# A chunked scan's triangular inverse: the last two doubling steps on small array tiles

## The chip, the cores and the metric

The kernel runs on one core of a Trainium2 chip, in float32 throughout. The metric is the device time of one execution in microseconds (us). A core has TensorE (PE in the profile; its weight loads are rows of their own, PEld), VectorE (DVE), ScalarE (ACT), GpSimd (POOL) and SyncE (SP), each with its own stream of instructions; they wait for each other through semaphores.

## The reference

The reference is two transformer-like blocks one after the other. The change lies in the first layer of the first block, in the part that computes the RWKV-7 recurrence of 8 heads of width 64 over 512 tokens (256 of context, 256 latent), once forwards and once backwards:

```
def step(S, r, w, k, v, a, b):
    S = S * w + (S @ a) outer b + v outer k      # one token
    y = S @ r
```

The kernel does not go token by token. It takes chunks of 128 tokens, and for each chunk and head it needs the inverse of a unit triangular matrix, (I - A)^-1, with A strictly triangular, 128x128. A is made of inner products of decayed keys.

## The kernel before, in words

**Units.** The scan is 16 units (`UNITS`): 2 directions x 4 chunks x 2 groups of four heads. One turn of the loop `for u, (d, c, pg) in enumerate(UNITS)` does unit u and prepares unit u+1. The same loop is written out three times, for PE, ACT and DVE, by hand; the order in each stream is the order of the code, and the semaphores `pe_done`, `act_done`, `vec_done` tell the engines how far the others are. SP issues no transfer that the scan waits for.

**The inverse.** All four heads of a unit are worked on, in two pairs p = 0 and 1. `ED` holds powers of the part of A inside 16x16 diagonal blocks, `TD` the growing inverse T; each has a plain half and a transposed half. `squared` and `grown` give the inverse within blocks of 16 (T1, T2, T4, T8). Then three doubling steps, lv = 0, 1, 2, go from blocks of 16 to 32, from 32 to 64 and from 64 to 128. Before the change each of them is the same: `bridge_mask` (DVE, L2451) multiplies A's transpose `dm` by a constant mask that leaves only the blocks which this step brings in, giving `bm[lv]`. `bridge` (PE, L983) multiplies that with T over the full 128x128 (Z, to banks 7 and 2), `bridge_out` (ACT, L1794) copies Z from PSUM to `zt`. `merged` (PE, L991, through `grown`, L970) multiplies Z with T, again over 128x128, and for lv = 1 in both the plain and the transposed form. `merged` on DVE (L2442) adds the product to T and writes it into the other buffer of `TD`. PE's pairs alternate: while ACT copies p = 0, PE computes p = 1.

A function `two` issues two products; each product of float32 operands is two weight loads and two matmuls in the trace. So `bridge` of one step and pair is 4 matmul records, at line L961, where `two` stands.

**Around it on PE, in one unit.** After step 0 come the products for x (L1036, L1041), then step 1, then `grams_a(u + 1)` (L949, four products of the next unit, at L955, with 64-row tiles), then step 2, then L1061 and L1065, and L1074, the first user of the finished inverse. On DVE, `masked` (L2388, rows at L2392), `masked_a` (L2396, rows at L2399) and `diagonal` (L2412) of the next unit stand between the steps. `bridge_mask(u + 1, 1)` and `bridge_mask(u + 1, 2)` stand at the end of the unit, behind the state (L2518) and ahead of the next unit's first `grown`.

Of the kernel before, what the change touches and what calls it, by code (L numbers as in the profile page):

```python
# [24 lines left out]
P = 128  # L25
# [195 lines left out]
class Counts:  # L221
# [16 lines left out]
    def at(self, engine, name):  # L238
        return 1 if self.known is None else self.known[engine, name]
# [12 lines left out]
def build(nc, w, out, counts, stop="end"):  # L252
# [5 lines left out]
    with ExitStack() as ctx:  # L258
# [137 lines left out]
        bm = [take(m, 4, P) for m in ("w0", "v", "ring 1")]  # L396
        zt = take("v", 4, P)
        POWER_BANK, GROW_BANK = (7, 2), (3, 4)

        def half_of(t, i, p, half):  # L400
            return cut(t[i][:, p, :], 256 * half, 2, P)
# [225 lines left out]
        def _(pe):  # L627
# [331 lines left out]
            def two(b, o, lhs, rhs):  # L959
                for m in range(2):  # L960
                    i = mm(bank[b][:, o + P * m:o + P * m + P], lhs[:, m, :], rhs[:, m, :],  # L961
                           start=True, stop=True, skip_group_check=True)
                return i
# [16 lines left out]
                for p in range(2):  # L980
                    squared("E2", u, p, 0)

            def bridge(u, lv, p):  # L983

                if p == 0:
                    pe.wait_ge(vec_done, at(VE, ("bm", u, lv)))
                pe.wait_ge(vec_done, at(VE, (("T8 turned", u, p), ("Tm turned", u, 0, p), ("Tm", u, 1, p))[lv]))
                two(POWER_BANK[p], 0, bm[lv][:, 2 * p:2 * p + 2, :], half_of(TD, 1 - lv % 2, p, 1)
                    ).then_inc(pe_done, did(PE, ("Z", u, lv, p)))

            def merged(u, lv, p):  # L991

                pe.wait_ge(act_done, at(AC, ("Z", u, lv, p)))
                z = zt[:, 2 * p:2 * p + 2, :]
                grown(("Tm", lv), u, p, z, 1 - lv % 2, ((0,), (0, 1), (1,))[lv])

            decays(0)
            by_token(0)
# [3 lines left out]
            for u, (d, c, pg) in enumerate(UNITS):  # L1002
# [21 lines left out]
                if not last:  # L1024
                    grams(u + 1)
                for p in range(2):
                    bridge(u, 0, p)
                for p in range(2):
                    merged(u, 0, p)


                pe.wait_ge(vec_done, at(VE, ("sin", u)))
# [13 lines left out]
                for p in range(2):  # L1046
                    bridge(u, 1, p)
                for p in range(2):
                    merged(u, 1, p)
                if not last:  # L1050
                    grams_a(u + 1)
                for p in range(2):
                    bridge(u, 2, p)
                for p in range(2):
                    merged(u, 2, p)


                if not last:
# [11 lines left out]
                for q in range(2):  # L1070
                    pe.wait_ge(vec_done, at(VE, ("Tm", u, 2, q)))
# [534 lines left out]
        def _(ac):  # L1606
# [55 lines left out]
            def copy(name, dst, src, scale=1.0):  # L1662
                act(dst, src, ACT.Copy, scale=scale).then_inc(act_done, did(AC, name))  # L1663
# [130 lines left out]
            def bridge_out(u, lv):  # L1794

                for p in range(2):
                    ac.wait_ge(pe_done, at(PE, ("Z", u, lv, p)))
                    copy(("Z", u, lv, p), zt[:, 2 * p:2 * p + 2, :], cut(bank[POWER_BANK[p]], 0, 2, P))

            decays(0)  # L1800
            out_of("bkt", 0, 5, bkt[0])
# [1 line left out]
            for u in range(len(UNITS)):  # L1803
                last = u + 1 == len(UNITS)
                if not last:
                    decays(u + 1)
                power_out("E4", u, 0)
                power_out("E8", u, 1)
                if not last:
                    out_of("bkt", u + 1, 5, bkt[(u + 1) % 2])  # L1810
                bridge_out(u, 0)
                ac.wait_ge(pe_done, at(PE, ("x", u)))
                copy(("xs", u), xs, cut(bank[0], 0, 2, P))
                bridge_out(u, 1)
                bridge_out(u, 2)
# [230 lines left out]
        def _(ve):  # L2046
# [395 lines left out]
            def merged(u, lv, p, before):  # L2442

                ve.wait_ge(vec_done, before)
                ve.wait_ge(pe_done, at(PE, (("Tm", lv), u, p)))
                o, e = ((0, 256), (0, 512), (256, 512))[lv]
                i = 1 - lv % 2
                V.tensor_tensor(TD[1 - i][:, p, o:e], TD[i][:, p, o:e], bank[GROW_BANK[p]][:, o:e], ALU.add
                                ).then_inc(vec_done, did(VE, ("Tm", u, lv, p)))

            def bridge_mask(u, lv):  # L2451

                off = wide(const(("off32", "off64", "off128")[lv])[:, None, :], 4, P)
                V.tensor_tensor(bm[lv], dm[u % 2], off, ALU.mult).then_inc(vec_done, did(VE, ("bm", u, lv)))

            for part in range(5):
                decayed(0, part)
# [5 lines left out]
            diagonal(0, 1)  # L2463
            for p in range(2):
                power_turned("E2", 0, p, 1)
            for lv in range(3):
                bridge_mask(0, lv)
            for u, (d, c, pg) in enumerate(UNITS):
                last = u + 1 == len(UNITS)
                grown("T2", u, 0, 0, at(VE, ("T1", u)))  # L2470
                power_turned("E4", u, 0, 0)
                if not last:
                    decayed(u + 1, 0)
                grown("T2", u, 1, 0, at(VE, ("T1", u)))
                power_turned("E4", u, 1, 0)
                if not last:
                    decayed(u + 1, 1)
                grown("T4", u, 0, 1, at(VE, ("T2", u, 0)))
                grown("T4", u, 1, 1, at(VE, ("T2", u, 1)))
                if not last:  # L2480
                    decayed(u + 1, 2)
                if not last:
                    decayed(u + 1, 3)
                for p in range(2):
                    grown("T8", u, p, 0, at(VE, ("T4", u, p)))
                    inverse_turned(("T8 turned", u, p), u, p, 1, at(VE, ("T8", u, p)))
                if not last:
                    decayed(u + 1, 4)
                if not last:
                    masked(u + 1, 0)  # L2490
                for p in range(2):
                    merged(u, 0, p, at(VE, ("T8", u, p)))
# [3 lines left out]
                for p in range(2):  # L2496
                    merged(u, 1, p, at(VE, ("Tm turned", u, 0, p)))
# [4 lines left out]
                for p in range(2):  # L2502
                    merged(u, 2, p, at(VE, ("Tm", u, 1, p)))
                if not last:
                    diagonal(u + 1, 1)
                    bridge_mask(u + 1, 0)
                    for p in range(2):
                        power_turned("E2", u + 1, p, 1)
                ve.wait_ge(pe_done, at(PE, ("s", u)))
                op(("s sum", u), V.tensor_tensor(stt_, sin_[u % 2], cut(bank[6], 0, 2, P), ALU.add))  # L2510
                for jj in range(2):
                    V.scalar_tensor_tensor(state[:, 4 * d + 2 * pg + jj, :], stt_[:, jj, :],
                                           ex[u % 2][:, jj, 257:258], const("head"), ALU.mult, ALU.mult
                                           ).then_inc(vec_done, did(VE, ("state 1" if jj else "state 0", u)))
                ve.wait_ge(pe_done, at(PE, ("y", u)))
                y_ = yt[:, c, 256 * pg:256 * pg + 256]
                if d == 0:
                    V.tensor_copy(y_, bank[5][:, 0:256]).then_inc(vec_done, did(VE, ("state", u)))  # L2518
# [426 lines left out]
```

## Time and profile before

| | |
|---|---|
| median of 3 runs | 3063.39 us (3062.32 to 3063.72) |
| the profiled execution, span from first to last instruction | 3062.6 us |
| runs' median beyond that span | 0.8 us |
| PE busy | 2955.8 us (97%) |
| one scan unit, period | 22.25 us |
| scan, units | 16, from about 340 to 697 us |

The profile is of one execution. A row of the timeline joins neighbouring instructions of an engine that have the same line and operands: its start, the time to the end of the last one, the engine, the line, the operation, and the count. What is in brackets is idle time of the engine ahead of the row and what ended it. A PE row's shape "128\*128" is the rows and columns of the array that its weights fill; "128x128" behind it is the moving operand and result.

### The profile page before, as it was taken

What the parts mean: (1) busy time and instruction counts of PE and PEld (TensorE: products, weight loads), DVE (VectorE), ACT (ScalarE), POOL (GpSimd) and SP (SyncE); (2) the same over time, 40 slices, a digit from 0 to 9 for tenths busy, and PEclk for the clock granted to TensorE, in tenths of its full rate; (3) what the DMA queues carried; (4) which work ended last, traced back from release to release, by engine and by line L of the source; (5) the groups of instructions that cost most, each with busy time, mean ns of one, the idle gap of its engine ahead of it and who ended that gap; (6) DMA issues with size and microseconds to landing.
All of it is one profiled execution on the core that took longest, in us unless ns stands there. A gap on an engine that the chain in (4) does not pass through costs nothing.

```text
span 3062.6 us, 50591 instructions
## 1 busy us (share of the span) xinstructions
PE 2955.8 (97%) x21484; PEld 1949.8 (64%) x21484; DVE 1315.0 (43%) x3016; ACT 541.7 (18%) x1202; POOL 14.0 (0%) x13
## 2 busy tenths in 40 slices
PE   7999899999999999999899999999999899999998
PEld 5554699994344444557754555544568678877887
DVE  1567888875998987404421111111121432023211
ACT  2213332321211111204300000000011310022000
POOL 0000100000000000000000000000000000000000
PEclk8999899999999999999999999999999999999999
DMA  7232001004777885320299999999962235522551
GB/s 270 95 138 82 1 1 42 1 15 132 230 237 232 246 255 181 135 82 15 84 358 384 378 371 372 374 396 382 377 241 97 83 97 151 151 83 69 151 151 55
DMA packets 351380, 551.02 MB, mean 180 GB/s; under 512 B 14304, under 2 KB 292192, under 8 KB 347840
## 3 DMA queue, kind: packets, MB, share of 16 engines
q1 hardware_dynamic: 351168, 547.89, 51.2%
q8 instruction: 170, 2.79, 0.4%
q14 instruction: 42, 0.34, 0.0%
HBM read 546.80 MB, written 1.05 MB: 179 GB/s over the span
## 4 chain that ended last, share of the span: by engine, by line
PE 91%; DVE 4%; ACT 2%; DMA 1%; issue 1%; SPq 0%; ACTq 0%; DVEq 0%
PE bank L678 16%; PE bank L1367 15%; PE bank L1159 8%; PE bank L1383 8%; PE bank L1560 7%; PE bank L961 7%; PE bank L1173 5%; PE bank L757 3%; PE bank L637 3%; PE bank L1200 2%; PE bank L1104 2%; PE bank L945 1%; DVE mix L2143 1%; PE bank L1234 1%; PE bank L1326 1%; PE bank L1315 1%
## 5 line engine op out<-in xcount | busy, mean ns | idle before, releaser
L678 PE MATMUL bank<-a,ring 128*128 128x256 f32 (+1 forms) x1792 | 451.5, 414 | 9.2 <-DVE a L2078 6.6
L2143 DVE SCALAR_TENSOR_TENSOR mix<-arena,csil,mix 128x256 f32<-128x256 f32 x1008 | 402.1, 482 | 31.3 <-ACT mix L1663 31.3
L678 PEld LDWEIGHTS bank<-a,ring 128*128 128x128 f32 x1792 | 340.7, 191 | 116.8 <-issue 64.6
L1367 PE MATMUL bank<-ring,arena 128*32 128x352 f32 x5376 | 402.1, 459 | 1.7 <-DVE small L2681 1.7
L1367 PEld LDWEIGHTS bank<-ring,arena 128*32 128x32 f32 x5376 | 179.5, 110 | 218.8 <-issue 194.8
L1159 PE MATMUL bank<-a,ring 128*128 128x512 f32 x704 | 307.6, 597 | 6.8 <-ACT a L1659 6.8
L1159 PEld LDWEIGHTS bank<-a,ring 128*128 128x128 f32 x704 | 133.2, 191 | 179.9 <-issue 177.9
L1560 PE MATMUL bank<-arena,ring 128*128 128x256 f32 x1024 | 223.5, 379 | 2.0 <-DVE arena L2865 2.0
L1383 PE MATMUL bank<-ring,arena 128*32 128x256 f32 x3840 | 213.3, 379 | 0.0
L1560 PEld LDWEIGHTS bank<-arena,ring 128*128 128x128 f32 x1024 | 194.4, 190 | 29.1 <-DVE arena L2865 2.8
L2748 DVE TENSOR_TENSOR arena<-arena,bank 128x352 f32<-128x352 f32 x48 | 25.0, 521 | 433.7 <-ACT arena L1932 433.7
L1663 ACT ACTIVATE arena<-bank 128x256 f32<-128x256 f32 (+1 forms) x303 | 128.0, 429 | 365.2 <-PE bank L961 137.2
L1383 PEld LDWEIGHTS bank<-ring,arena 128*32 128x32 f32 x3840 | 125.3, 110 | 82.3 <-issue 3.7
L1173 PE MATMUL bank<-arena,ring 128*128 128x512 f32 x352 | 152.6, 593 | 1.5 <-DVE arena L2557 1.5
L2846 DVE TENSOR_SCALAR tmpA<-bank,mods 128x256 f32<-128x256 f32 x32 | 15.5, 484 | 288.0 <-PE bank L1560 213.9
L961 PE MATMUL bank<-arena 128*128 128x128 f32 x896 | 125.4, 285 | 3.9 <-DVE arena L2420 2.1
L1173 PEld LDWEIGHTS bank<-arena,ring 128*128 128x128 f32 x352 | 66.7, 190 | 86.4 <-issue 84.1
L961 PEld LDWEIGHTS bank<-arena 128*128 128x128 f32 x896 | 110.1, 193 | 16.5 <-ACT arena L1663 7.7
L1612 ACT ACTIVATE mix<-a 128x256 f32<-128x256 f32 x64 | 21.9, 417 | 526.5 <-DVE a L2058 526.5
L1663 ACT ACTIVATE mix<-arena,csil 128x256 f32<-128x256 f32 x144 | 64.2, 498 | 238.5 <-DMA arena<-in_ada_w 144.4
L757 PE MATMUL bank<-a,ring 128*128 128x512 f32 (+1 forms) x224 | 99.0, 594 | 0.0
L2861 DVE TENSOR_SCALAR tmpA<-bank 128x256 f32<-128x256 f32 x64 | 27.2, 425 | 164.3 <-PE bank L678 164.3
(422 smaller groups left out, 3203.4 us busy)
## 6 DMA issues: line engine op xcount, KB each, us to landing
ring<-in_moe_w SPq DMA_DIRECT2D x224, 704.0 KB, 9.2
ring<-in_moe_w SPq DMA_DIRECT2D x160, 512.0 KB, 6.5
ring<-in_mlp_w SPq DMA_DIRECT2D x64, 1024.0 KB, 5.5
arena<-in_ada_w SPq DMA_DIRECT2D x96, 512.0 KB, 3.7
arena<-in_w_ada SPq DMA_DIRECT2D x48, 512.0 KB, 3.6
ring<-in_ffn_w SPq DMA_DIRECT2D x22, 1024.0 KB, 8.4
arena<-in_moe_w SPq DMA_DIRECT2D x32, 704.0 KB, 10.0
h<-in_w_ada SPq DMA_DIRECT2D x8, 2048.0 KB, 7.6
```

What stands on the lines that cost most here:

```text
L637: i = mm(bank[b][:, 0:tile.shape[-1]], const("mean"), tile, start=(k == 0), stop=(k == KT - 1))
L678: i = mm(bank[b][:, 0:n], ws[:, k, t * P:t * P + P], rhs[:, k, sl], start=(k == 0), stop=(k == KT - 1))
L757: i = mm(bank[RKV_BANK[n]][0:m, :], ws[:, k, n % 2 * P:n % 2 * P + m], aT[:, k, :], start=(k == 0), stop=(k == KT - 1), skip_group_check=True)
L961: i = mm(bank[b][:, o + P * m:o + P * m + P], lhs[:, m, :], rhs[:, m, :], start=True, stop=True, skip_group_check=True)
L1104: i = mm(bank[MIX_BANKS[j % 5]], ws[:, k, j % 2 * P:j % 2 * P + P], src, start=(k == 4), stop=(k == 3), skip_group_check=True)
L1159: i = mm(bank[2 * t + i_], ws[:, k, t * P:t * P + P], aT[:, k, :], start=(k == 0), stop=(k == KT - 1))
L1173: i = mm(bank[2 + n % 4], ws[:, k, :], G[:, k, :], start=(k == 0), stop=(k == FT - 1))
L1367: i = mm(b[32 * t:32 * t + 32, 0:PART], ac_[:, g, 32 * k:32 * k + 32], by_tile(ws[i_], t), start=(k == 0), stop=(k == KT - 1), skip_group_ ...
L1383: i = mm(bank[Y_BANKS[g]][32 * q:32 * q + 32, 0:256], gT[:, p, g, 32 * c:32 * c + 32], ws[:, 256 * q:256 * q + 256], start=(n == 0), stop= ...
L1560: j = mm(bank[4 + n % 2][:, 0:TL], ws[:, k, :], G2[:, 16 * half + k, :], start=(half + k == 0), stop=(half * k == 15))
L1663: act(dst, src, ACT.Copy, scale=scale).then_inc(act_done, did(AC, name))
L2143: ins = V.scalar_tensor_tensor(dst, x, cond, dst, ALU.mult, ALU.add)
```

## The change

Step 0 stays as it was. Steps 1 and 2 are replaced. T after step 0 has nonzero blocks only in 32x32 diagonal blocks, and what step 1 adds to it is two 32x32 blocks; step 2 adds one 64x64 block. `blocks_of` gives, for a level, the pairs (on, by) of row and column ranges. `bridge_blocks` multiplies only such blocks of `dm` (no mask) and T; `merged_blocks` multiplies only the blocks of T and Z. `block_products` issues the four heads of one block pair one after the other, all on the same array tile. For step 1 the rows and columns are 32 wide: 8 products for Z, 12 for T (8 of one form, 4 of the transposed form of the first block, which step 2 needs). For step 2 they are 64 wide: 4 and 4. The four heads go to one PSUM bank, so there is no longer a pair p = 0 and a pair p = 1: one semaphore count tells that all of Z is done, and one that all of T's products are. ACT copies Z's blocks (two copies for step 1, one for step 2). DVE copies the new blocks into their place in the same buffer of `TD` (three copies for step 1, one for step 2), with no addition. The masks `bm` for steps 1 and 2 and their buffers go.

```
-            def bridge(u, lv, p):
+            def bridge(u, p):
...
+            def block_products(b, out_rows, out_cols, lhs, rhs):
+                for h in range(4):
+                    i = mm(bank[b][out_rows, P * h + out_cols.start:P * h + out_cols.stop], lhs(h), rhs(h),
+                           start=True, stop=True, skip_group_check=True)
+                return i
...
+            def bridge_blocks(u, lv):
+                if lv == 1:
+                    for p in range(2):
+                        pe.wait_ge(vec_done, at(VE, ("Tm turned", u, 0, p)))
+                else:
+                    pe.wait_ge(vec_done, at(VE, ("Tm", u, 1)))
+                for by, on in blocks_of(u, lv):
+                    i = block_products(BRIDGE_BANK[lv], on, by, lambda h: dm[u % 2][by, h, on],
+                                       lambda h: inverse_at(h, 1, by, by))
+                i.then_inc(pe_done, did(PE, ("Z", u, lv)))
+
+            def merged_blocks(u, lv):
+                pe.wait_ge(act_done, at(AC, ("Z", u, lv)))
+                for by, on in blocks_of(u, lv):
+                    i = block_products(4, on, by, lambda h: inverse_at(h, 0, on, on), lambda h: zt[on, h, by])
+                if lv == 1:
+                    by, on = blocks_of(u, 1)[0]
+                    i = block_products(3, by, on, lambda h: zt[on, h, by], lambda h: inverse_at(h, 0, on, on))
+                i.then_inc(pe_done, did(PE, ("Tm", u, lv)))
...
+            def bridge_blocks_out(u, lv):
+                ac.wait_ge(pe_done, at(PE, ("Z", u, lv)))
+                for n, (by, on) in enumerate(blocks_of(u, lv)):
+                    copy(("Z", u, lv) if n == 2 - lv else ("Z part", u, lv), zt[on, :, by],
+                         cut(bank[BRIDGE_BANK[lv]], 0, 4, P)[on, :, by])
...
+            def merged_blocks(u, lv):
+                ve.wait_ge(pe_done, at(PE, ("Tm", u, lv)))
+                pieces = [(1, 4, on, by) for by, on in reversed(blocks_of(u, lv))]
+                if lv == 1:
+                    by, on = blocks_of(u, 1)[0]
+                    pieces.insert(1, (0, 3, by, on))
+                for n, (half, b, rows_, cols_) in enumerate(pieces):
+                    V.tensor_copy(whole(TD, 0, half)[rows_, :, :, cols_], cut(bank[b], 0, 2, 2, P)[rows_, :, :, cols_]
+                                  ).then_inc(vec_done, did(VE, ("Tm", u, lv) if n + 1 == len(pieces)
+                                                           else ("Tm part", u, lv, n)))
...
-                if not last:
-                    bridge_mask(u + 1, 1)
-                    bridge_mask(u + 1, 2)
                 ve.wait_ge(vec_done, now(VE))
```

How the streams stand now. On PE, between the products for x and the first user of the finished inverse, before (two instructions of the trace for each product):

```order
L1036 MATMUL bank<-ring 128x128
L1041 MATMUL bank<-arena,h 128x64 x2
L961 MATMUL bank<-ring,arena 128x128 x6
L961 MATMUL bank<-arena,ring 128x128 x2
L961 MATMUL bank<-ring,arena 128x128 x2
L961 MATMUL bank<-arena,ring 128x128 x2
L955 MATMUL bank<-arena 128x128 x4
L961 MATMUL bank<-arena,ring 128x128 x4
L961 MATMUL bank<-arena 128x128 x4
L1061 MATMUL bank<-ring 128x128
```

and the same place in the changed kernel, where L1077 is the old L1036, L964 the old L955 and L1098 the old L1061:

```order
L1077 MATMUL bank<-ring 128x128
L1082 MATMUL bank<-arena,h 128x64 x2
L1008 MATMUL bank<-ring 32x32 x8
L1008 MATMUL bank<-arena,ring 32x32 x8
L1008 MATMUL bank<-ring,arena 32x32 x4
L964 MATMUL bank<-arena 128x128 x4
L1008 MATMUL bank<-ring 64x64 x4
L1008 MATMUL bank<-arena,ring 64x64 x4
L1098 MATMUL bank<-ring 128x128
```

The 12 products of step 1 and the 8 of step 2 have become 20 and 8. None has moved past another group.

On DVE, from the next unit's masked products to the end of the unit, before:

```order
L2392 TENSOR_TENSOR arena<-bank,consts 128x512 x2
L2448 TENSOR_TENSOR arena<-ring,bank 128x512 x2
L2399 TENSOR_TENSOR arena<-bank,consts 128x256 x2
L2416 TENSOR_TENSOR arena<-arena,consts 128x2x256
L2448 TENSOR_TENSOR ring<-arena,bank 128x256 x2
...
L2518 COPY ring<-bank 128x256
L2454 TENSOR_TENSOR arena<-arena,consts 128x512
L2454 TENSOR_TENSOR ring<-arena,consts 128x512
L2434 TENSOR_TENSOR arena<-ring,bank 128x256
```

and now, where L2500 is the new copy, L2442 the old L2399, L2459 the old L2416 and L2477 the old L2434:

```order
L2435 TENSOR_TENSOR arena<-bank,consts 128x512 x2
L2500 COPY ring<-bank 32x2x2x32 x3
L2442 TENSOR_TENSOR arena<-bank,consts 128x256 x2
L2459 TENSOR_TENSOR arena<-arena,consts 128x2x256
L2500 COPY ring<-bank 64x2x2x64
...
L2568 COPY ring<-bank 128x256
L2477 TENSOR_TENSOR arena<-ring,bank 128x256
```

The two additions of each step have become three copies and one, and the two masks (L2454) ahead of the next unit's first addition are gone.

## Rows read from the trace of the kernel before

**Rows 1.** The page, part 1: busy time, share of the span, instructions.

```profile
PE 2955.8 (97%) x21484; PEld 1949.8 (64%) x21484; DVE 1315.0 (43%) x3016; ACT 541.7 (18%) x1202; POOL 14.0 (0%) x13
```

**Rows 2.** Busy time by engine in a stretch of one unit.

```profile
core 0: us, PE busy (x) PEld busy (x) DVE busy (x) ACT busy (x) POOL busy (x), PEclk, DMA share, GB/s
409.60:431.90 22.30, 22.22 (x186) 20.65 (x185) 18.58 (x44) 7.03 (x20) 0.00 (x0) 1.00 0.01 2
```

**Rows 3.** Waits in the unit from 409.2 to 431.4: total us, times, longest.

```profile
ACT arena L1663 <- PE bank L961: 7.8, 6, 3.0
PEld bank L961 <- ACT arena L1663: 0.7, 3, 0.2
```

**Rows 4.** Timeline of PE's weight loads, steps 1 and 2 of that unit.

```profile
420.23 0.97 PEld L961 LDWEIGHTS bank<-ring,arena 128*128 128x128 f32 x8
421.43 0.52 PEld L961 LDWEIGHTS bank<-ring,arena 128*128 128x128 f32 x4 [0.22 <-ACT arena L1663]
...
422.76 0.53 PEld L961 LDWEIGHTS bank<-arena,ring 128*128 128x128 f32 x4
423.41 0.52 PEld L955 LDWEIGHTS bank<-arena 64*128 64x128 f32 x8
...
425.24 0.97 PEld L961 LDWEIGHTS bank<-arena 128*128 128x128 f32 x8 [0.22 <-ACT arena L1663]
426.12 0.30 PEld L1061 LDWEIGHTS bank<-ring 128*128 128x128 f32 x2
```

**Rows 5.** Timeline of DVE in the same unit, with one row of ACT's (420.99).

```profile
409.19 0.42 DVE L2518 COPY ring<-bank 128x256 f32<-128x256 f32 x1
409.53 0.68 DVE L2454 TENSOR_TENSOR arena<-ring,consts 128x512 f32<-128x512 f32 x1
410.12 0.68 DVE L2454 TENSOR_TENSOR ring<-ring,consts 128x512 f32<-128x512 f32 x1
410.84 0.42 DVE L2434 TENSOR_TENSOR arena<-ring,bank 128x256 f32<-128x256 f32 x1
...
420.06 0.45 DVE L2440 STREAM_TRANSPOSE ring<-ring 128x256 f32<-128x256 f32 x1
...
420.99 0.83 ACT L1663 ACTIVATE arena<-bank 128x256 f32<-128x256 f32 x2
...
422.69 0.69 DVE L2448 TENSOR_TENSOR arena<-ring,bank 128x512 f32<-128x512 f32 x1 [1.01 <-PE bank L961]
426.06 0.87 DVE L2448 TENSOR_TENSOR ring<-arena,bank 128x256 f32<-128x256 f32 x2 [0.52 <-PE bank L961]
...
431.44 0.42 DVE L2518 COPY ring<-bank 128x256 f32<-128x256 f32 x1
```

**Rows 6.** Groups by form, the scan from 343.9 to 697: count, busy us, mean ns.

```profile
L961 PE MATMUL bank<-ring,arena 128*128 128x128 f32 x508 | 75.0, 280 | 0.5
L1663 ACT ACTIVATE mix<-bank 128x256 f32<-128x256 f32 x32 | 12.3, 384 | 81.1 <-PE bank L1074 47.7 <-PE bank L1041 33.4
L1781 ACT ACTIVATE arena<-bank 128x128 f32<-128x128 f32 x28 | 7.9, 284 | 0.0
L2384 DVE TENSOR_SCALAR ring<-mix,arena 128x128 f32<-128x128 f32 x30 | 6.6, 264 | 0.0
```

**Rows 7.** Narrow weights elsewhere: a page group of the expert stage, and a timeline.

```profile
L1383 PE MATMUL bank<-ring,arena 128*32 128x256 f32 x3840 | 213.3, 379 | 0.0
...
L1383 PEld LDWEIGHTS bank<-ring,arena 128*32 128x32 f32 x3840 | 125.3, 110 | 82.3 <-issue 3.7
...
792.96 1.07 PE L1135 MATMUL bank<-mix,consts 128*32 128x512 f32 x8
792.96 0.16 PEld L1135 LDWEIGHTS bank<-mix,consts 128*32 128x32 f32 x8 [0.76 <-DVE mix L2143]
```

**Rows 8.** The same view, from 763 us on: a pause of PE, and the stretch behind it.

```profile
763.00:767.00 4.00, 0.74 (x2) 0.00 (x0) 2.53 (x2) 0.63 (x1) 0.00 (x0) 1.00 1.08 366
767.00:773.80 6.80, 3.28 (x4) 1.51 (x5) 6.42 (x9) 4.52 (x10) 0.00 (x0) 0.51 1.10 349
```

More of the change, by code:

```diff
@@ L395, in build, with blocks_of @@
         TD = [take(m, 2, 512) for m in ("ring 1", "lora")]
-        bm = [take(m, 4, P) for m in ("w0", "v", "ring 1")]
+        bm = take("w0", 4, P)
         zt = take("v", 4, P)
         POWER_BANK, GROW_BANK = (7, 2), (3, 4)
+        BRIDGE_BANK = (None, 7, 2)
+        def blocks_of(u, lv):
+            n, late = 32 * lv, UNITS[u][0] == 0
+            pairs = [(slice(2 * n * b + n, 2 * n * b + 2 * n), slice(2 * n * b, 2 * n * b + n))
+                     for b in range(P // (2 * n))]
+            return pairs if late else [(on, by) for by, on in reversed(pairs)]
         def half_of(t, i, p, half):
@@ L981, in squares @@
                     squared("E2", u, p, 0)
-            def bridge(u, lv, p):
+            def bridge(u, p):
                 if p == 0:
[L986 to L995, printed above, removed]
+                    pe.wait_ge(vec_done, at(VE, ("bm", u)))
+                pe.wait_ge(vec_done, at(VE, ("T8 turned", u, p)))
+                two(POWER_BANK[p], 0, bm[:, 2 * p:2 * p + 2, :], half_of(TD, 1, p, 1)
+                    ).then_inc(pe_done, did(PE, ("Z", u, 0, p)))
@@ new lines, in merged, with inverse_at @@
+            def merged(u, p):
+                pe.wait_ge(act_done, at(AC, ("Z", u, 0, p)))
+                grown(("Tm", 0), u, p, zt[:, 2 * p:2 * p + 2, :], 1)
+            def block_products(b, out_rows, out_cols, lhs, rhs):
[3 more added lines that the diff above has]
+                return i
+            def inverse_at(h, half, rows_, cols_):
+                return half_of(TD, 0, h // 2, half)[rows_, h % 2, cols_]
@@ L1026, in _ @@
                 for p in range(2):
-                    bridge(u, 0, p)
+                    bridge(u, p)
                 for p in range(2):
-                    merged(u, 0, p)
+                    merged(u, p)
                 pe.wait_ge(vec_done, at(VE, ("sin", u)))
@@ L1045, in _ @@
                 i.then_inc(pe_done, did(PE, ("x", u)))
[L1046 to L1049, printed above, removed]
+                bridge_blocks(u, 1)
+                merged_blocks(u, 1)
                 if not last:
                     grams_a(u + 1)
[L1052 to L1055, printed above, removed]
+                bridge_blocks(u, 2)
+                merged_blocks(u, 2)
                 if not last:
@@ L1069, in _ @@
                 pe.wait_ge(act_done, at(AC, ("xs", u)))
-                for q in range(2):
-                    pe.wait_ge(vec_done, at(VE, ("Tm", u, 2, q)))
+                pe.wait_ge(vec_done, at(VE, ("Tm", u, 2)))
                 for jj in range(2):
@@ L1792, in power_out, with bridge_out @@
                     copy((name, u, p), ED[i][:, p, 0:256], bank[POWER_BANK[p]][:, 0:256])
-            def bridge_out(u, lv):
+            def bridge_out(u):
                 for p in range(2):
-                    ac.wait_ge(pe_done, at(PE, ("Z", u, lv, p)))
-                    copy(("Z", u, lv, p), zt[:, 2 * p:2 * p + 2, :], cut(bank[POWER_BANK[p]], 0, 2, P))
+                    ac.wait_ge(pe_done, at(PE, ("Z", u, 0, p)))
+                    copy(("Z", u, 0, p), zt[:, 2 * p:2 * p + 2, :], cut(bank[POWER_BANK[p]], 0, 2, P))
+            def bridge_blocks_out(u, lv):
[3 more added lines that the diff above has]
+                         cut(bank[BRIDGE_BANK[lv]], 0, 4, P)[on, :, by])
             decays(0)
@@ L1810, in _ @@
                     out_of("bkt", u + 1, 5, bkt[(u + 1) % 2])
-                bridge_out(u, 0)
+                bridge_out(u)
                 ac.wait_ge(pe_done, at(PE, ("x", u)))
                 copy(("xs", u), xs, cut(bank[0], 0, 2, P))
-                bridge_out(u, 1)
-                bridge_out(u, 2)
+                bridge_blocks_out(u, 1)
+                bridge_blocks_out(u, 2)
                 ac.wait_ge(pe_done, at(PE, ("u", u)))
@@ L2440, in inverse_turned, with merged, bridge_mask @@
                 V.transpose(TD[i][:, p, 256:512], TD[i][:, p, 0:256]).then_inc(vec_done, did(VE, name))
-            def merged(u, lv, p, before):
+            def merged(u, p, before):
                 ve.wait_ge(vec_done, before)
[L2445 to L2454, printed above, removed]
+                ve.wait_ge(pe_done, at(PE, (("Tm", 0), u, p)))
+                V.tensor_tensor(TD[0][:, p, 0:256], TD[1][:, p, 0:256], bank[GROW_BANK[p]][:, 0:256], ALU.add
+                                ).then_inc(vec_done, did(VE, ("Tm", u, 0, p)))
+            def merged_blocks(u, lv):
[8 more added lines that the diff above has]
+                                                           else ("Tm part", u, lv, n)))
+            def bridge_mask(u):
+                V.tensor_tensor(bm, dm[u % 2], wide(const("off32")[:, None, :], 4, P), ALU.mult
+                                ).then_inc(vec_done, did(VE, ("bm", u)))
             for part in range(5):
@@ L2465, in _ @@
                 power_turned("E2", 0, p, 1)
-            for lv in range(3):
-                bridge_mask(0, lv)
+            bridge_mask(0)
             for u, (d, c, pg) in enumerate(UNITS):
@@ L2491, in _ @@
                 for p in range(2):
-                    merged(u, 0, p, at(VE, ("T8", u, p)))
+                    merged(u, p, at(VE, ("T8", u, p)))
                     inverse_turned(("Tm turned", u, 0, p), u, p, 0, at(VE, ("Tm", u, 0, p)))
@@ L2495, in _ @@
                     masked(u + 1, 1)
-                for p in range(2):
-                    merged(u, 1, p, at(VE, ("Tm turned", u, 0, p)))
+                merged_blocks(u, 1)
                 if not last:
@@ L2501, in _ @@
                     diagonal(u + 1, 0)
-                for p in range(2):
-                    merged(u, 2, p, at(VE, ("Tm", u, 1, p)))
+                merged_blocks(u, 2)
                 if not last:
                     diagonal(u + 1, 1)
-                    bridge_mask(u + 1, 0)
+                    bridge_mask(u + 1)
                     for p in range(2):
```

## The prediction

> **What bounds the kernel now.** I read the page first: PE is busy for 97% of the span [rows 1]. That alone doesn't say that fewer products are worth anything, so I went to the scan. One of its units, read between two copies of the same kind on DVE, lasts 431.44 - 409.19 = 22.25 us [rows 5]. In such a stretch PE is busy for 22.22 of 22.30 us, DVE for 18.58 and ACT for 7.03, at the full granted clock of 2.4 GHz (1.00) [rows 2]. The waits say the same from the other side: ACT waits for PE 7.8 us in a unit, while PE's weight loads wait for ACT 0.7 us [rows 3]. So PE's stream sets the scan's time, and a product taken from it is worth its own pace unless a wait takes its place.
>
> That pace: eight loads of 128 columns take 0.97 us, of which the last alone is 0.19, so a record follows the one before by (0.97 - 0.19) / 7 = 0.11 us [rows 4]. Loading hides behind multiplying. The stretch that the change rewrites runs from the first load of step 1 at 420.23 to the first load of L1061 at 426.12: **5.89 us** in each unit, 26% of it. In it are 40 records of the two steps (4.5 us), eight of L955, two waits for ACT of 0.22 us, and two changes of tile shape. A change costs 0.20 us: the loads at 422.76 end at 423.29, the next of the same shape would have begun 0.08 us before that end, and the one of L955 begins 0.12 after it [rows 4].
>
> **What is removed and what is added.** Of PE, 20 products of 128x128 (40 records) go, and 20 of 32x32 and 8 of 64x64 come (56 records). No operation with a 32x32 or 64x64 tile is in the trace, so their pace is the unknown. Its lower bound is what 32 columns take. At L1383 four column tiles work at once, each record of 256 columns comes 213.3 / 3840 = 0.0555 us after the last, so one tile streams 256 columns in 0.222 us and 32 columns in 0.028 [rows 7]. Weights of 32 columns don't ask for more: at L1135 eight loads for four tiles take 0.16 us, two to a tile [rows 7]. The upper bound that the rows of busy tiles allow is 0.0555 us, since L1383 proves that the queue can issue load and matmul at least so often. I take 0.028: at L1135 the eight loads, each 0.11 long, begin within 0.16 - 0.11 = 0.05 us, so the issue itself can be faster still. For 64 columns it is 0.056.
>
> The other prices. A result is there when its matmul ends: 0.28 us at 128 columns, 0.38 at 256 [rows 6, 7], so 0.20 at 32 and 0.23 at 64. From an engine's end to the next one's start I count 0.04 to 0.05 us: ACT's first copy begins at 420.99 and takes 0.38, and the load that waits for it begins at 421.43 [rows 4, 5]. A copy on ACT takes 0.28 us for 128 elements of each partition and 0.38 for 256 [rows 6]; on DVE 0.42 for 256 from PSUM [rows 5], and for 128 between 0.26 (from SBUF) [rows 6] and 0.42; I take 0.29, since 512 elements (0.69) and 256 (0.42) differ by 0.27 [rows 5], which makes 0.13 for 128 elements less. A second copy behind a first one, of the same engine, adds 0.17 on ACT and 0.21 on DVE, because it starts before the first ends, as the two masks do (0.59 apart at 0.68 each) [rows 5]. That only 32 or 64 partitions take part saves nothing.
>
> **The new stretch step by step**, in us of the same unit:
>
> - Step 1 now needs both pairs of T at once. DVE ends the second transposition at 420.51 [rows 5], so the first load is at 420.56 instead of 420.23 and the first matmul at 420.59. (The change of shape, 0.20, lies inside this wait.) Z, 16 records: last one 0.42 later, 421.01, result 421.21.
> - ACT's two copies: 421.25 to 421.70. PE loads at 421.75. Here PE stands still for 0.7 us; before, the second pair filled this.
> - T's products, 24 records from 421.78: last 422.42, result 422.62. DVE's three copies: 422.66 to 423.37.
> - L955: a change of shape, first load 422.54, matmuls from 422.65 to 422.99. It hides part of DVE's copies. The next load would be at 423.19; it waits for DVE until 423.42.
> - Z of step 2, 8 records from 423.47: last 423.86, result 424.09. ACT 424.13 to 424.51. PE loads at 424.56, its second long pause.
> - T's products of step 2: 424.61 to 425.00, a change of shape, and L1061's load at **425.15** instead of 426.12.
>
> So 4.5 us of records become about 2.0, the pauses on PE grow by some 1.3 us (0.33 at the start, 0.7 and 0.5 for ACT, 0.23 for DVE, less the two of 0.22), one more change of shape is seen, and the unit gains **0.97 us**. Does anything else take it back? DVE's copy of the last block ends at about 425.7; L1074 wants it at 425.15 + 1.34 = 426.49. DVE loses two masks of 0.68 each, and of its additions (1.38 and 0.87 busy) what the copies (0.71 and 0.42) don't take, over 2 us of 18.6: it can't become the bound. The masks stood ahead of the next unit's first addition at 410.84, which began with no idle time before it [rows 5]. PE hardly waited for that addition, so I count 0.03 us for their going, between 0 and 0.1. Together 1.0 us in each of 16 units: **16 us**. Behind the scan everything hangs on its end, and its transfers are released by it, so the gain arrives whole. The profiled execution would go from 3062.6 to 3046.6 us; its span lies 0.8 below the median of the runs, so the median goes from 3063.4 to **3047.4 us**.
>
> One rule speaks for a smaller gain. The Trainium skill (TensorEngine Tiling, Key Properties) says that changing the tiling mode drains TensorE; the trace agrees, with the 0.20 us above, and two changes in a unit become four. In my chain the two new ones fall into waits or are counted.
>
> **Rivals.**
>
> *Tiles overlap (3037 us).* The four heads of a block share one array tile, but the next block has another. L1135 runs its four tiles side by side (8 records of 0.59 us in 1.07 [rows 7]), where neighbours in the program are on different tiles. If PE also reaches past four products of one tile, Z of step 1 lasts 8 records instead of 16 and T's products 8 instead of 24: 24 x 0.028 = 0.67 us less, 1.65 in a unit, 26.4 us. Against it: nothing in this trace shows it reach so far. The TensorE page (Part 3, The mechanism) has matmuls in strict order and only loads pulled ahead, which would forbid it.
>
> *A floor on small records (about 3063 us).* If a 32x32 record takes 0.0555 us, the 15 + 23 steps between them cost 1.04 us more and nothing is left: 0.0 a unit. The skill (TensorE: Matmul & The Clock Gate, Wait — 56ns, not 53.3ns?) has a floor of 62 ns for a matmul that its sequencer handles in software; that mechanism here would be 38 x 0.034 = 1.3 us a unit more than my sum, 3068 us. The eight loads of L1135 that begin within 0.05 us speak against a floor. Of this rival's chance I give a quarter to that rule.
>
> *Records of one tile don't overlap (slower, about 3097 us).* Every tiled product of the kernel before has a neighbour on another tile. If, on one small tile, a load can't be hidden behind the matmul before it, a record takes the whole load of 32 columns, 0.110 us [rows 7]. Then 38 x 0.082 = 3.1 us a unit come on top: 2.1 us slower, 34 in all. It decides from 0.064 us a record on. Against it: at 128*128 the neighbours do share a tile, and there 0.11 is less than the 0.19 of a load.
>
> *The clock.* PE was granted 1.2 GHz (0.51) after a stretch in which it worked for 0.74 of 4.00 us [rows 8]. The new pauses are 0.7 us at most with work between them, yet a 32x32 tile is little work. A fifth of each unit at half clock would cost over 2 us and undo the gain.
>
> **How the numbers follow.** My forecast has 45%, the overlapping tiles 22%, the floor 17%, the tile without overlap 10%, the clock 6%. A measurement of this kernel can tell 0.2%, 6 us, from no change. The first two are faster (with a tail of the floor at 0.04 us a record): 0.71. The floor is the same: 0.15. The last two: 0.14. The range must leave out no more than two in ten: 3035, just past the overlapping tiles, to 3067, past the floor.
>
> **What would show it.** The period between the DVE copies should be 21.2 us. Rows of 32x32 records should have 16 in about 0.6 us and 24 in about 0.85; an ACT wait of PE of about 0.5 us, twice; a DVE wait ahead of the 64x64 products of 0.2. Records 0.055 or 0.11 us apart prove the rivals, and 16 records in 0.4 us the overlap. The masks' rows should be 16, not 48. The granted clock should stay at 1.00.

## The result, and the profile after

| | before | after |
|---|---|---|
| median | 3062.86 us (3061.47 to 3063.72, 4 runs) | 3126.41 us (3125.38 to 3128.35, 4 runs) |
| ratio, 95% interval | | 1.0209 (1.0196 to 1.0221): slower, by about 2% |
| span of the profiled execution | 3062.6 us | 3124.0 us |
| mean granted clock, share of full speed | 0.986 | 0.958 |
| mean period of a scan unit | 22.12 us | 25.81 us |

The change makes the kernel 63.6 us slower by the medians, where 16 us faster was forecast. Each of the 16 units ends with DVE writing y: a copy in the first eight (L2568), an addition in the others (L2570). Of the 61.4 us by which the spans differ, 55.3 lie between the first and the last of these 16 writes (387.1 instead of 331.8 us), 1.3 ahead of them and 4.8 behind, where the clock is low for 60.0 us instead of 46.1.

The page of the changed kernel, busy times and the granted clock in 40 slices (the first of these answers to [rows 1]; the scan is in slices 5 to 10):

```profile
PE 2992.2 (96%) x21740; PEld 1982.5 (63%) x21740; DVE 1283.2 (41%) x2984; ACT 531.3 (17%) x1186; POOL 14.0 (0%) x13
...
PEclk8999878878999999999989999999999999999999
```

PE is busy *longer* than before, 2992.2 against 2955.8 us, although 40 wide records of each unit gave way to 56 small ones. The slices that read 7 and 8 say why. The same in windows, columns as in [rows 2]: two neighbouring stretches of one unit, then 320 us of the scan.

```profile
391.90:405.40 13.50, 12.62 (x131) 11.46 (x131) 10.02 (x25) 4.81 (x14) 0.00 (x0) 1.00 0.01 1
405.50:419.00 13.50, 13.03 (x76) 12.44 (x72) 6.44 (x15) 1.53 (x4) 0.00 (x0) 0.50 0.00 1
...
340.00:660.00 320.00, 300.88 (x2470) 279.95 (x2469) 204.19 (x499) 79.38 (x225) 0.00 (x0) 0.81 0.03 11
```

In the first stretch PE runs at 2.4 GHz and does 131 records; in the second it is *more* busy (13.03 of 13.50 us) and does 76, in part of other kinds, at 1.2 GHz. The clock falls around step 1 or 2 of a unit and comes back some 7 to 14 us later. Between the first and the last of the DVE writes it is low for 156.6 us, in the kernel before for none. PE's weight loads show the price of a product at both levels. Those of the changed kernel, first eight 128x128 loads in a low stretch, then those of steps 1 and 2 in a unit at full clock, answering to [rows 4]:

```profile
413.70 1.83 PEld L970 LDWEIGHTS bank<-arena 128*128 128x128 f32 x8
...
482.39 0.48 PEld L1008 LDWEIGHTS bank<-ring 32*32 32x32 f32 x16 [0.32 <-DVE ring L2483]
483.62 0.41 PEld L1008 LDWEIGHTS bank<-arena,ring 32*32 32x32 f32 x14 [0.76 <-ACT arena L1699]
...
484.29 0.52 PEld L964 LDWEIGHTS bank<-arena 64*128 64x128 f32 x8
485.37 0.54 PEld L1008 LDWEIGHTS bank<-ring 64*64 64x64 f32 x8 [0.55 <-DVE ring L2500]
486.51 0.54 PEld L1008 LDWEIGHTS bank<-arena,ring 64*64 64x64 f32 x8 [0.60 <-ACT arena L1699]
487.12 0.33 PEld L1098 LDWEIGHTS bank<-ring 128*128 128x128 f32 x2
```

Eight loads take 1.83 us in the low stretch instead of the 0.97 of [rows 4]. The steps themselves came out nearly as worked out: the longest pause in this unit is 0.76 us, and from the end of the second transposition (481.83 + 0.45 = 482.28, in DVE's rows below) to L1098's load it takes 4.84 us, where the forecast had 4.64 (425.15 - 420.51).

```profile
481.83 0.45 DVE L2483 STREAM_TRANSPOSE ring<-ring 128x256 f32<-128x256 f32 x1
...
484.40 0.91 DVE L2500 COPY ring<-bank 32x128 f32<-32x128 f32 x3 [0.96 <-PE bank L1008]
```

### The profile page after: what moved, and what is told of

It reads as the page before. It is cut to its first block, busy times and chain, and to the rows that moved or that the text cites. A ratio compares the mean times of both kernels' runs of the same rounds, so it can differ in the third digit from the quotient of the medians.

```text
span 3124.0 us, 50975 instructions
## 1 busy us (share of the span) xinstructions
PE 2992.2 (96%) x21740; PEld 1982.5 (63%) x21740; DVE 1283.2 (41%) x2984; ACT 531.3 (17%) x1186; POOL 14.0 (0%) x13
## 4 chain that ended last, share of the span: by engine, by line
PE 90%; DVE 5%; ACT 2%; DMA 1%; issue 1%; SPq 0%; DVEq 0%; ACTq 0%
PE bank L687 16%; PE bank L1403 15%; PE bank L1195 8%; PE bank L1419 7%; PE bank L1596 7%; PE bank L1209 5%; PE bank L970 4%; PE bank L766 3%; PE bank L646 3%; PE bank L1236 2%; PE bank L1140 2%; PE bank L1008 2%; DVE mix L2186 1%; PE bank L954 1%; PE bank L1110 1%; PE bank L1270 1%
## 5 line engine op out<-in xcount | busy, mean ns | idle before, releaser
L1699 ACT ACTIVATE arena<-bank 128x256 f32<-128x256 f32 (+3 forms) x287 | 117.8, 417 | 375.5 <-PE bank L687 131.2
```

## The experiments

Two readings of the fall were open. **Pauses**: PE now stands still four times in a unit for 0.2 to 0.8 us, and that alone lowers the clock, whatever the products are. **Small tiles**: time in which PE works on a 32x32 tile counts for little, so that pauses and small products together look like standing still. The expectations call the first reading A and the second B; the first of them has a third, C: the loss is the length of the pauses, and not the clock's. Unless said otherwise a time is of one run, with one of the kernel before beside it on the same chip; the unit's period and the time at 1.2 GHz are of the profiled run, between the first and the last of the DVE writes (15 periods, called units below, the last of which is some 2 us shorter than the others where the clock is full).

**Wide products in the pauses.** Ahead of each of the four waits PE multiplies a constant identity with a constant, over the full 128x128, into a bank that nobody uses at that time. Such a product is called a filler: one, two, one and one of them.

```
+            def fill(b, n):
+
+                for _ in range(n):
+                    mm(bank[b][:, 0:P], ident, const("cs128", P), start=True, stop=True, skip_group_check=True)
...
             def bridge_blocks(u, lv):
+                fill(2, 1 if lv == 1 else 1)
...
             def merged_blocks(u, lv):
+                fill(2 if lv == 1 else 7, 2 if lv == 1 else 1)
                 pe.wait_ge(act_done, at(AC, ("Z", u, lv)))
```

> The changed kernel with products on the full array put into PE's pauses (1, 2, 1 and 1 products of 128x128 ahead of the four waits of steps 1 and 2; they write a bank that nobody reads). Nothing is left out. Theory A (the pauses of PE lower the granted clock): the clock stays at 1.00 in the scan and the time falls to about 3048 us. Theory B (products on small tiles count for little work, however long PE is busy with them): the fillers give some work back, the clock still falls in many units, about 3070 to 3110 us. Theory C (the loss is not the clock's but the pauses' own length): 3126 us or more.

Measured: **3052.5 us** beside 3064.3. The period is 21.51 to 21.54 us in 14 of 15 units, the clock low for 9.1 us, in the last one.

```profile
340.00:660.00 320.00, 318.64 (x3131) 289.89 (x3130) 243.88 (x595) 94.00 (x266) 0.00 (x0) 1.00 0.05 15
```

Added work for nothing, 5 products in each unit, takes 74 us off the changed kernel. So the whole loss is the clock's, and C is out. A's figure was 3048; B's on record, 3070 to 3110 with the clock still falling, was missed. B can only stand if a few wide products are enough to hold the clock, which was not said beforehand. So this run does not decide. It does rule out the changes of tile shape as the cause: with the fillers there are more of them, and the clock holds.

**Same pauses, no small tile.** The changed kernel's order, waits, copies and pauses, with all 20 products of steps 1 and 2 over the full array.

```
+            EVERY = slice(0, P)
...
+                if lv in (1, 2):
+                    i = block_products(BRIDGE_BANK[lv], EVERY, EVERY, lambda h: dm[u % 2][:, h, :],
+                                       lambda h: inverse_at(h, 1, EVERY, EVERY))
...
+                if lv in (1, 2):
+                    i = block_products(4, EVERY, EVERY, lambda h: inverse_at(h, 0, EVERY, EVERY), lambda h: zt[:, h, :])
+                    if lv == 1:
+                        i = block_products(3, EVERY, EVERY, lambda h: zt[:, h, :], lambda h: inverse_at(h, 0, EVERY, EVERY))
```

> The structure of the changed kernel (four heads together, the same waits, the same copies in place, no masks), but each product of steps 1 and 2 over 128x128 of the array: 20 products as before the change instead of 28 small ones. The pauses of PE stay as they are in the changed kernel. At full clock the longer products make a unit some 1.6 us longer than before the change: 3088 us. Theory B: 3088 us with the clock at 1.00. Theory A: the clock falls as in the changed kernel, 3120 us or more.

Measured: **3095.2 us** beside 3064.3, period 24.14 to 24.17, never at 1.2 GHz in the scan. Its windows, and its waits from 345 to 690 us:

```profile
340.00:660.00 320.00, 297.58 (x2437) 274.65 (x2436) 216.85 (x532) 85.68 (x243) 0.00 (x0) 1.00 0.04 11
```

```profile
PEld bank L1010 <- ACT arena L1710: 21.0, 28, 0.8
```

The same wait in the changed kernel:

```profile
PEld bank L1008 <- ACT arena L1699: 18.0, 26, 0.8
```

PE waits for ACT twice in a unit, as in the changed kernel, and no shorter (0.75 us each on average, 0.69 there), and is busy for *less* of the 320 us (297.6 against 300.9), at full clock. Pauses of that size alone don't lower it. (3088 was expected. Of the other 7 us, some 0.3 lie in each unit, 24.15 instead of 23.85, and 3.0 behind the scan.)

**One step at a time.** Only step 1, or only step 2, over the full array.

> As the changed kernel, with step 1 (32 to 64) on the full array and step 2 (64 to 128) on 64x64 tiles. At full clock about 3070 us. Theory A: the clock falls about as often as in the changed kernel. Theory B: the clock falls less, since only 16 of the 56 small records are left and they are on a quarter of the array; 3070 to 3090 us.

> As the changed kernel, with step 1 on 32x32 tiles and step 2 on the full array. At full clock about 3062 us. Theory A: the clock falls about as often as in the changed kernel, 3120 us or more. Theory B: the clock falls, but less than with both steps small, 3080 to 3110 us.

Measured: 3102.5 us with only step 2 on 64x64 tiles (34.1 us at 1.2 GHz, in 5 of 15 units), 3096.0 with only step 1 on 32x32 tiles (72.1 us, in 10 of 15). With both small it is 156.6. Each by itself is enough for a fall in some units, fewer than in the changed kernel, as B has it; for step 2 alone B's range, 3070 to 3090, was missed by 12 us. Units that the fall spares take 23.4 and 22.25 us.

**Small products in the pauses.** As the first experiment, with the fillers on one 32x32 tile, and more of them (2, 7, 3, 3), so that they last about as long as the wide ones.

```
+                    mm(bank[b][0:32, 0:32], ident[0:32, 0:32], const("cs128", 32)[0:32, :], start=True, stop=True, skip_group_check=True)
```

> The changed kernel with PE's pauses filled like in e1_fill, for about as long, but with products on one 32x32 tile (2, 7, 3 and 3 of them). Nothing is left out. Theory A (what lowers the clock is that PE stands still): the clock holds as in e1_fill, about 3053 us. Theory B (what counts is how much of the array works, small tiles give little): the clock falls as often as in the changed kernel, 3120 us or more.

Measured: **3137.9 us** beside 3059.5, at 1.2 GHz for 176.6 us.

```profile
340.00:660.00 320.00, 314.89 (x2758) 292.76 (x2758) 197.37 (x479) 76.98 (x218) 0.00 (x0) 0.78 0.04 11
```

This is the row that decides against A, which had 3053. PE is busy for 314.9 of 320 us, 98%; among the kernels here only the one before the change (318.9) and those that wide fillers keep at full clock have more. Yet its granted clock, 0.78, is the lowest of all. PE's busy time does not tell the clock when the tiles are small.

One thing no run separates: in every small product here the tile and the number of moving columns shrink together (32x32 weights with 32 columns, 64x64 with 64). "Small tile" stands for both.

**Fewer wide fillers.** Only those ahead of the two waits for ACT, two and one.

> e1_fill with fillers only in the two waits for ACT (2 products of 128x128 ahead of step 1's T, 1 ahead of step 2's), so 3 instead of 5. Theory B: a unit at full clock is about 21.3 us; if three fillers are enough to hold the clock, 3048 us; if not, between 3053 and 3126 us.

Measured: 3091.4 us. Units of 21.5 to 21.7 us (6 of the first 14) stand beside units of 24.7 and 26.2; 86.8 us low. The fall isn't a fixed price of the code but happens in some units and not in others, and less wide work makes it more frequent: 8 of the first 14 units here, none with five fillers, all with none.

**Useful work in the first ACT pause.** Half of the products for y (jj = 0 of L1098 and L1102) moves from behind step 2 to between `bridge_blocks(u, 1)` and `merged_blocks(u, 1)`. DVE masks `kb` ahead of `bb` for q = 1, so that these products don't wait.

```
                 bridge_blocks(u, 1)
+                if not last:
+                    pe.wait_ge(vec_done, at(VE, ("kb", u + 1, 1)))
+                for jj in (0,):
...
                 merged_blocks(u, 1)
...
-                for jj in range(2):
+                for jj in (1,):
...
-                for name, b, dst in (("bb", (6, 1)[q], bb), ("kb", (0, 5)[q], kb)):
+                both = (("bb", (6, 1)[q], bb), ("kb", (0, 5)[q], kb))
+                for name, b, dst in (both if q == 0 else reversed(both)):
```

> The changed kernel with half of the products for y (three of the six products at L1098 and L1102) moved from behind step 2 into the wait for ACT in step 1; DVE copies bank 5 of the next unit's masked products first, so that they can start. No filler, all the work real. At full clock a unit would be about 20.8 us, 3040 us in all. Theory B: the same work in less time on the same few columns, so the clock still falls, though the stretch of small tiles is broken up: 3060 to 3120 us. Theory A: the longest pause is gone, one of 0.5 us is left, the clock holds: 3040 us.

> e6_early_y with one product of 128x128 as a filler ahead of each of the two waits of step 2. Theory B: the clock holds if two fillers and the moved products are enough; then 3042 us, else up to 3090 us. Theory A: 3042 us.

Measured: 3090.2 us for the move alone, every unit 23.90 with a low stretch of about 7 us. With one wide filler ahead of each of the two waits of step 2, **3040.2 us** beside 3059.5; 3042 was expected.

The row of windows with the fillers, PE's timeline around the moved products and the fillers, and DVE's copies at the end of two units following each other (423.48 - 402.58 = 20.90 us):

```profile
340.00:660.00 320.00, 315.33 (x3109) 287.98 (x3108) 250.11 (x612) 97.40 (x276) 0.00 (x0) 1.00 0.05 15
```

```profile
414.53 0.49 PE L1098 MATMUL bank<-ring 128*128 128x128 f32 x2
414.86 0.56 PE L1102 MATMUL bank<-arena,h 128*128 128x64 f32 x4
...
416.66 0.49 PE L1019 MATMUL bank<-consts 128*128 128x128 f32 x2
...
417.69 0.49 PE L1019 MATMUL bank<-consts 128*128 128x128 f32 x2
```

```profile
402.58 0.42 DVE L2584 COPY ring<-bank 128x256 f32<-128x256 f32 x1
...
423.48 0.42 DVE L2584 COPY ring<-bank 128x256 f32<-128x256 f32 x1
```

Its period is 0.6 us below that of the first experiment, since a pause of 0.76 us now holds products that the unit needs. L1019 is the filler.

**Between these.** The move with step 2 over the full array and no filler, and the move with one filler, ahead of the second ACT wait.

> e6_early_y with step 2 on the full array instead of 64x64 tiles: real products take the place of fillers. At full clock 20.8 + 0.9 us for 16 longer records - 0.3 for two changes of tile shape: 21.4 us a unit, 3050 us. Theory B: the 32x32 records are all the small work that is left, the clock holds or nearly so: 3050 to 3065 us.

> e7_early_y_fill with one filler instead of two, the one ahead of step 2's T. At full clock 20.8 us a unit, 3040 us. Theory B: e7 holds the clock and e6 loses it in every unit, this lies between; 3040 us if one filler is enough, up to 3090 if not.

Measured: 3074.7 us (35.5 us low; 3050 to 3065 was expected) and 3083.9 (92.0 us low). In both, units at full clock (21.8 and 20.9 us) and fallen ones (up to 26.2 and 25.4) mix. Both lie between the extremes in wide work; neither is safe.

**Long pauses.** Does the length of a pause matter by itself? The kernel with full products and the changed order again, with four useless copies on ACT, one after the other, ahead of each `bridge_blocks_out`. PE's two ACT pauses become 2.5 and 2.3 us.

```
                 ac.wait_ge(pe_done, at(PE, ("Z", u, lv)))
+                for n in range(4):
+                    copy(("idle", u, lv, n), zt[:, :, 0:64], cut(bank[BRIDGE_BANK[lv]], 0, 4, P)[:, :, 0:64])
+                    ac.wait_ge(act_done, at(AC, ("idle", u, lv, n)))
```

> e2_full_tiles (all products on the full array) with PE's two waits for ACT made longer: four more copies of 256 elements on ACT ahead of the real ones in each of steps 1 and 2, one behind the other, about 1.7 us each time, so that PE stands still some 2.4 and 2.2 us. At full clock 24.1 + 3.4 = 27.5 us a unit, about 3147 us. Theory B in its wide form (the clock follows the work the full array gets done, whatever the reason that it is low): the clock falls too, 3160 to 3250 us. Theory B in its narrow form (only small tiles lower it): clock held, 3147 us.

Then the same pauses filled: with 32 and 28 products on a 32x32 tile, and with 9 and 8 over the full array.

> e9_long_pauses with its two pauses a unit filled with products on one 32x32 tile (32 and 28 of them, about 2.0 and 1.8 us). All other products are on the full array. If work on a small tile counts like standing still, the clock is as in e9: 3165 to 3185 us, most units at full clock. If a 32x32 product counts for its time, the clock never falls: 3147 us. If such products lower the clock more than a pause does, 3200 us and more.

> e9_long_pauses with its two pauses filled with products over the full array (9 and 8 of 128x128, about 2.0 and 1.8 us). The clock never falls in the scan: 3147 to 3155 us, on either reading of e13.

| | us | kernel before beside it | at 1.2 GHz between the DVE writes |
|---|---|---|---|
| long pauses, empty | 3173.9 | 3062.6 | 45.4 us |
| with small products | 3165.0 | 3062.0 | 31.7 us |
| with wide products | 3142.0 | 3062.0 | 0 |

The rows of windows, of the three kernels in this order:

```profile
340.00:660.00 320.00, 265.41 (x2058) 245.32 (x2058) 183.04 (x448) 106.10 (x294) 0.00 (x0) 0.95 0.03 11
```

```profile
340.00:660.00 320.00, 309.00 (x3461) 287.51 (x3460) 189.87 (x465) 108.20 (x300) 0.00 (x0) 0.98 0.04 11
```

```profile
340.00:660.00 320.00, 305.44 (x2542) 284.83 (x2541) 191.12 (x470) 109.19 (x301) 0.00 (x0) 1.00 0.04 11
```

Long pauses do lower the clock in some units (10 of the first 14 stay at 27.45 us; two falls, each across two units, make the others 31.8 and 29.0), so a pause isn't harmless. But with 17% of the 320 us empty the clock is 0.95, where small products at 98% busy had 0.78. Filling the pauses with small products brings PE from 83% to 97% busy and leaves units falling (5 of the first 14); filling them with wide ones, at 95% busy, ends it. It lies between the two readings, nearer to small products counting as nothing: they may count a little, and one run of each can't tell a little from chance. The kernel with wide products came out 5 us below its range of 3147 to 3155.

**The best of these, measured again.** The kernel with the early half of y and two fillers, in five rounds.

> e7_early_y_fill again, now timed against the kernel before. Theory B: 3040 us, ratio 0.992 to 0.994, with every unit but the last at full clock.

Measured: median **3046.88 us** (3038.77 to 3049.43, 5 runs) against 3062.57 (9 runs) for the kernel before, ratio **0.9944** (0.9931 to 0.9958). It beats both kernels, the changed one by 2.5%, and falls just short of what was expected (3040 us, 0.992 to 0.994). The single run above was 3040.2; the two profiles have the same scan (20.9 us a unit), and differ behind it, 2364.3 and 2370.6 us from the last DVE write to the end. There the clock is low for 43.3 us in the one and for 56.4 in the other, which makes up most of the difference at the price found below, 0.43 us for each. Of the five runs the one of 3038.8 has a mean granted clock of 0.986, the others 0.982 or 0.983. Why the clock behind the scan differs between runs of one kernel stays open.

## Why the prediction was wrong

**What bounds the kernel: right, and part of the trap.** PE's stream sets the scan's time; every time above follows it. But the argument priced PE's stream in records, at one clock.

**The step that failed: the clock stays at 1.00.** The sum used full-clock durations throughout, and the rival "The clock" was given 6%, because the new pauses were 0.7 us at most, against a stretch with 0.74 us of work in 4.00 in [rows 8]. The pauses were sized rightly (0.76 at most), and the experiment with the same pauses and no small tile shows that they alone do not lower it. What was missed is the other half of that rival's own sentence, that a 32x32 tile is little work: together, the pauses and the tiles leave the stretch with so little work on the whole array that the clock falls in each of the 15 units. The rival's size was too small as well. It took a fifth of each unit at half clock, for over 2 us; the trace has 10.4 of 25.8 us low. At full clock the 15 periods would last about 15 x 21.5 - 2 = 320 us, from the first experiment's period; they last 387, so the clock costs 67 us, or 4.4 a unit. The range ended at 3067 and left out both slower rivals, so the time lies far outside it.

The Trainium skill (TensorE: Matmul & The Clock Gate, What's actually happening) says the gate goes by how busy PE has been lately. Between kernels with wide products the trace agrees (1.00 at 95% busy, 0.95 at 83%); at 98% busy on small tiles with a granted 0.78 it doesn't, if busy means what the profile counts.

**The gain at full clock: right in kind, 0.2 us too large.** Forecast 0.97 us a unit for the stretch; measured 0.77 (the 4.84 us of the timeline, less the 5.61 from 420.51 to 426.12 in [rows 4, 5]). The term that was too small is the second copy behind a first one, taken to overlap it (0.17 us more on ACT, 0.21 on DVE). These copies, unlike the masks of [rows 5], follow each other without overlap: ACT's two took 0.56 us instead of 0.45, so T's first load came 0.1 late, and DVE's three took 0.91 us instead of 0.71, so step 2 began 0.18 late.

```profile
483.02 0.56 ACT L1699 ACTIVATE arena<-bank 32x128 f32<-32x128 f32 x2 [0.38 <-PE bank L1008]
```

In the first experiment units that keep the clock take 21.51 to 21.54 us, 0.7 less than the 22.25 of before, where the forecast had 21.2. With the clock kept, the gain of 16 us would by this estimate have been some 12. (The chances of the prediction don't quite add up either: the last two rivals had 10 and 6%, and count as 0.14 at its end.)

**The rivals on the tiles fell.** Sixteen 32x32 loads in 0.48 us, the last one alone 0.11, are 0.025 us apart on average; the forecast took 0.028. So there is no floor at 0.0555, and no missing overlap on one tile. The average hides two things: on one tile the matmuls start first 0.028 and then 0.032 us apart, somewhat more than the forecast's 0.028, and where the next tile begins, the records of both run side by side for a moment. The Trainium skill (TensorE: Matmul & The Clock Gate, Wait — 56ns, not 53.3ns?) has about 25 ns as the least distance of two matmuls' starts. On one tile the trace agrees; on two tiles it doesn't, where starts come 0.005 us apart.

Tiles do overlap, but little. PE's timeline of the changed kernel, T's products of step 1: 16 records of the plain form (arena,ring), which stand first in the program, and 8 of the transposed form (ring,arena), on the other tile.

```profile
404.94 0.49 PE L1008 MATMUL bank<-arena,ring 32*32 32x32 f32 x13 [0.65 <-ACT arena L1699]
405.24 0.21 PE L1008 MATMUL bank<-ring,arena 32*32 32x32 f32 x1
405.27 0.19 PE L1008 MATMUL bank<-arena,ring 32*32 32x32 f32 x1
405.30 0.19 PE L1008 MATMUL bank<-ring,arena 32*32 32x32 f32 x1
```

The first record of the second form starts ahead of the last three of the first. All 24 take 0.84 us here, where the clock falls on the way (at 405.4), and 0.74 in the unit at full clock, from 483.63; 0.85 was forecast, and 0.4 would be the full overlap.

**The masks.** L2506 has 16 rows instead of 48, as forecast, and DVE never became the bound.

## What to carry to other kernels

On a kernel that PE bounds, cutting useless columns from products also cuts what keeps TensorE's clock up: before small array tiles replace wide ones in the middle of a dense stream, look for wide work to put between them, and read the granted clock of the stretch, not PE's busy share. Useful products moved into the waits are best, and where there are none, a few wide products into a bank that is free just then can pay for themselves many times over. How many it takes has to be measured: here five held the clock in all but the last unit and three didn't, and with useful products in the longest wait two held it and one didn't. A kernel in which units fall now and then is near the edge, and one run of it says little.

## What the runs showed of the hardware

- Products of 32x32 with 32 moving columns count for little in what sets TensorE's clock: 0.78 granted at 98% busy with them in the pauses, where full-array products in the same places gave 1.00 at 99.6%. Whether the tile or the few columns make it so was not separated. Whether 64x64 tiles count in part stays open; with them alone in step 2 the clock fell in 5 of 15 units.
- Long pauses are tolerated better than I thought: 2.5 and 2.3 us empty in each unit of 27.5 left 10 of the first 14 units at full clock, in a kernel whose scan works on wide tiles otherwise.
- The fall costs 0.43 us for each us spent at 1.2 GHz (67 of 156.6, an estimate that takes the unit at full clock from the first experiment), somewhat less than the half that a stream bound by the array alone would lose; eight 128x128 loads take 1.83 us there instead of 0.97.
- Matmuls on different tiles may start in another order than the program has. The Trainium skill (TensorE: Matmul & The Clock Gate, The mechanism) has them in strict order; the rows above don't agree: a record on the next tile starts ahead of three that stand before it in the program.
